# Two orders of TensorE work changed: the matmuls that open an mLSTM head, and two projections that close the token mixing

## The reference

```python
log_w = jnp.where(causal, b[..., :, None] - b[..., None, :] + ig[..., None, :], -jnp.inf)
m_t = jnp.maximum(log_inter, jnp.max(log_w, -1))
w = jnp.exp(log_w - m_t[..., None])
qk = jnp.einsum('bhtd,bhsd->bhts', q, k) * w
```

```python
y = y * lax.rsqrt(jnp.mean(y * y, axis=-1, keepdims=True) + RMS_EPS)
y_ret = (jax.nn.silu(rg) * y) @ w_ret_out
y_na = _neighborhood_attention(na_heads(nq), na_heads(nk), na_heads(nv), rel_bias) @ w_na_out
merged = jax.nn.sigmoid(g_ret) * y_ret + jax.nn.sigmoid(g_na) * y_na
return merged @ w_out
```

## Time and profile before

| | us |
|---|---|
| median of 3 runs | 2721.13 (2720.45 to 2722.01) |
| profiled execution, its own time | 2721.13 |
| its span | 2719.3 |
| TensorE busy (PE) | 2637.1 |
| TensorE weight loads (PEld) | 2344.3 |
| VectorE busy (DVE) | 1584.0 |
| ScalarE busy (ACT) | 1396.6 |

### The profile page before, as it was taken

One profiled execution on the slowest core, in us unless ns is written; L12 is line 12 of the kernel. 1 busy time (PEld: TensorE's weight loads), 2 busy tenths in 40 slices (PEclk: granted clock), 3 DMA queues, 4 the chain that ended last, 5 costly groups with the idle time before them and its releaser, 6 DMA issues.

```text
span 2719.3 us, 46153 instructions
## 1 busy us (share of the span) xinstructions
PE 2637.1 (97%) x16650; PEld 2344.3 (86%) x16650; DVE 1584.0 (58%) x2847; ACT 1396.6 (51%) x2310; POOL 585.7 (22%) x336
## 2 busy tenths in 40 slices
PE   8999999999999998999999999999999999989998
PEld 6789999998888876799999998888869977766996
DVE  3558746675555563449556665555556646545664
ACT  4434567664444444444577654444445445553543
POOL 0007876650000000008866630000000000001000
PEclk9999999999999999999999999999999999999999
DMA  6245554446666653245544446666556655425554
GB/s 215 77 156 171 184 156 140 141 145 200 192 193 193 193 185 110 87 148 183 180 148 140 142 153 204 193 193 193 193 163 196 184 172 178 138 88 163 163 183 149
DMA packets 124037, 447.63 MB, mean 165 GB/s; under 512 B 14280, under 2 KB 14920, under 8 KB 123648
## 3 DMA queue, kind: packets, MB, share of 16 engines
q1 hardware_dynamic: 119808, 434.16, 50.8%
q0 software_dynamic: 2608, 9.08, 1.2%
q10 hardware_dynamic: 1488, 2.59, 0.3%
HBM read 444.74 MB, written 1.05 MB: 164 GB/s over the span
## 4 chain that ended last, share of the span: by engine, by line
PE 92%; DVE 4%; ACT 3%; DMA 1%; issue 1%; ACTq 0%; DVEq 0%
PE ps L748 41%; PE ps L720 14%; PE ps L726 14%; PE ps L723 14%; PE ps L896 4%; DVE X L1574 1%; PE ps L672 1%; PE ps L950 1%; PE ps L867 1%; DVE big L1574 1%; PE ps L782 0%; DMA ring<-in_ffn_in 0%; ACT w_hi L395 0%; DVE stats L1654 0%; DVE X L1650 0%
## 5 line engine op out<-in xcount | busy, mean ns | idle before, releaser
L395 ACT CAST w_hi<-ring 128x1024 fp32r<-128x1024 f32 (+1 forms) x808 | 846.4, 1048 | 999.1 <-PE ps L748 534.3
L407 DVE TENSOR_TENSOR w_lo<-ring,w_hi 128x1024 fp32r<-128x1024 f32 (+1 forms) x629 | 769.2, 1223 | 813.6 <-ACT w_hi L395 805.4
L407 POOL TENSOR_TENSOR w_lo<-ring,w_hi 128x1024 fp32r<-128x1024 f32 (+1 forms) x179 | 429.3, 2399 | 1713.5 <-ACT w_hi L395 1713.5
L720 PE MATMUL ps<-x_hi,w_hi 128*128 128x256 f32 x3104 | 772.8, 287 | 1.7 <-ACT w_hi L395 1.6
L723 PE MATMUL ps<-x_lo,w_hi 128*128 128x256 f32 x3104 | 760.6, 283 | 0.0
L720 PEld LDWEIGHTS ps<-x_hi,w_hi 128*128 128x128 f32 x3104 | 594.1, 191 | 3.3 <-ACT w_hi L395 2.1
L723 PEld LDWEIGHTS ps<-x_lo,w_hi 128*128 128x128 f32 x3104 | 594.9, 192 | 0.0
L726 PE MATMUL ps<-x_hi,w_lo 128*128 128x256 f32 x3104 | 435.7, 283 | 0.0
L748 PE MATMUL ps<-w_hi,x_hi 128*128 128x512 f32 x1488 | 409.7, 394 | 6.0 <-DVE x_lo L1621 1.9
L748 PE MATMUL ps<-w_hi,x_lo 128*128 128x512 f32 x1488 | 404.0, 390 | 0.0
L748 PE MATMUL ps<-w_lo,x_hi 128*128 128x512 f32 x1488 | 402.9, 389 | 0.3 <-DVE w_lo L407 0.3
(11 more groups left out here) (239 smaller groups left out, 1903.2 us busy)
## 6 DMA issues: line engine op xcount, KB each, us to landing
ring<-in_u SPq DMA_DIRECT2D x256, 512.0 KB, 3.5
ring<-in_v SPq DMA_DIRECT2D x256, 512.0 KB, 3.8
ring<-in_ffn_in SPq DMA_DIRECT2D x88, 512.0 KB, 3.5
ring<-in_ffn_out SPq DMA_DIRECT2D x44, 512.0 KB, 3.4
ring<-in_wq SPq DMA_DIRECT2D x32, 512.0 KB, 3.5
ring<-in_ple_gate SPq DMA_DIRECT2D x16, 512.0 KB, 4.3
SC<-in_rows POOLq DMA_DIRECT2D x11, 512.0 KB, 4.8
ring<-in_a_qk SPq DMA_DIRECT2D x8, 512.0 KB, 4.8
```

Of the source, the lines that this page charges most:

```text
L395: nc.scalar.copy(part(w_hi, i)[:, used(name)], tile(i)[:, used(name)]).then_inc(tiles_hi, 1)
L407: eng.tensor_tensor(part(w_lo, i)[:, at], tile(i)[:, at], part(w_hi, i)[:, at], ALU.subtract).then_inc(tiles_low[LOW[n][0]], 1)
L720: mm = nc.tensor.matmul(bank(s)[:, 0:T], hi[:, k, :], x_hi[:, k, :], start=(k == 0), stop=False)
```

## The change

There are two edits.

In `ml_first` the six matmuls are the same, in another order: each half of the decay is followed at once by its mask, the decay bank is reported full, and the scores come last. The second half of the decay now starts its own accumulation.

At the close of the mixing, `ret_out` comes before `na_out`: in the list of loads, in the order of `acc`, and on TensorE, ScalarE and VectorE. ScalarE loads the square root's table (`sqrt_table`: a table load and an activation of one column) before it casts the last tile of `g_na` and tile 0 of `ret_out`, and takes the eight roots before the sigmoid of `g_na`.

```diff
-    + [("na_out", 4), ("ret_out", 8), ("mix_out", 8)]
+    + [("ret_out", 8), ("na_out", 4), ("mix_out", 8)]
...
-             "na_out", "ret_out", "mix_out", "ffn2_out"]
+             "ret_out", "na_out", "mix_out", "ffn2_out"]
...
-                decay, scores = SLOT[("ml", "decay", h)], SLOT[("ml", "scores", h)]
-                slot_free(pe, decay)
-                nc.tensor.matmul(bank(decay)[:, 0:T], ml_sel[0:H8, h, :], ml_rows[0:H8, 7, :], start=True, stop=False)
-                nc.tensor.matmul(bank(decay)[:, T:T + P], ml_sel[0:H8, h, :], ml_rows[0:H8, 7, P:T],
-                                 start=False, stop=False)
-                slot_free(pe, scores)
+                s = SLOT[("ml", "decay", h)]
+                slot_free(pe, s)
+                nc.tensor.matmul(bank(s)[:, 0:T], ml_sel[0:H8, h, :], ml_rows[0:H8, 7, :], start=True, stop=False)
+                nc.tensor.matmul(bank(s)[:, 0:P], ident[:], ml_mask[:], start=False, stop=True)
+                nc.tensor.matmul(bank(s)[:, T:T + P], ml_sel[0:H8, h, :], ml_rows[0:H8, 7, P:T],
+                                 start=True, stop=False)
+                full(nc.tensor.matmul(bank(s)[:, T:T + P], ident[:], ml_mask[:], start=False, stop=True), s)
+                s = SLOT[("ml", "scores", h)]
+                slot_free(pe, s)
                 r, q, k = head_rows(h), h // 2, 4 + h // 2
-                nc.tensor.matmul(bank(scores)[:, 0:T], ml_qk[r, k, 0:P], ml_qk[r, q, :], start=True, stop=True)
-                full(nc.tensor.matmul(bank(scores)[:, T:T + P], ml_qk[r, k, P:T], ml_qk[r, q, P:T],
-                                      start=True, stop=True), scores)
-                nc.tensor.matmul(bank(decay)[:, 0:P], ident[:], ml_mask[:], start=False, stop=False)
-                full(nc.tensor.matmul(bank(decay)[:, T:T + P], ident[:], ml_mask[:], start=False, stop=True), decay)
+                nc.tensor.matmul(bank(s)[:, 0:T], ml_qk[r, k, 0:P], ml_qk[r, q, :], start=True, stop=True)
+                full(nc.tensor.matmul(bank(s)[:, T:T + P], ml_qk[r, k, P:T], ml_qk[r, q, P:T],
+                                      start=True, stop=True), s)
...
+            turn_over("ret", ret_y.rearrange("p t h n -> p t (h n)"))
+            split_to_acc("ret_out", turn="ret")
             moved(pe, SLOT[("na", "out", H8 - 1)])
             to_acc("na_out", tokens(na_oT), 4)
-            turn_over("ret", ret_y.rearrange("p t h n -> p t (h n)"))
-            split_to_acc("ret_out", turn="ret")
...
-                    take_high(act, "g_na", 2 * h + 1)
+                    sqrt_table()
+                    highs("g_na", 2 * h + 1, 2 * h + 2, following="ret_out")
...
+            square_roots(8)
             from_acc("g_na", lambda tb: sig_na[:, tb, :], ACT.Sigmoid)
-            square_roots(8)
-            take_high(act, "ret_out", 0)
             turned_parts("ret")
             highs("ret_out", 1, 8, following="mix_out")
+            acc_here(act, "na_out")
...
-            def gated_from(name, dst, gate):
-
+            turned_parts("ret")
+            lows("ret_out", 1, 8)
+            for name, dst, gate in (("ret_out", merged_tmp, sig_ret), ("na_out", merged, sig_na)):
                 for tb in range(TB):
                     acc_here(dve, name, tb)
                     V.tensor_tensor(dst[:, tb, :], gate[:, tb, :], acc_rows(tb), ALU.mult).then_inc(acc_moved, 1)
-
-            acc_moved_up_to("g_na", TB - 1)
-            gated_from("na_out", merged, sig_na)
-            turned_parts("ret")
-            lows("ret_out", 1, 8)
-            gated_from("ret_out", merged_tmp, sig_ret)
-            acc_moved_up_to("ret_out", TB - 1)
+            acc_moved_up_to("na_out", TB - 1)
```

## The result

The changed kernel takes 2736.89 us (median of 4 runs, 2735.34 to 2738.02) beside 2720.79 us of the kernel before: ratio 1.0053, 95% interval 1.0041 to 1.0066, so it is slower. The medians are 16.1 us apart; the ratio takes in nine more runs of the changed kernel (2729.89 to 2738.33) and stands for 14.4 us. In a second set of runs it was 2736.85 beside 2722.87, ratio 1.0053 (1.0038 to 1.0068). I had forecast +8.6 us and a range up to 2733.5. A few executions far outside all others (2806 us and more) are left out of every ratio and mean.

What follows compares the result with a forecast made beforehand. TensorE, busy for 97% of the span, was taken to bound the kernel. +5.1 us in the mLSTM heads and +3.5 us at the close of the mixing made +8.6 on 2721.13: 2729.7 us, range 2723.5 to 2733.5.

Steps and rivals of the forecast that it cites:

- Part 1, the toll: mLSTM heads (ml_first): three more changes of array rows a head, 0.20 us each at full clock; +5.1 us in all.
- The term for head 0: First mLSTM head, at the lower clock: three more changes of array rows at 0.30 us each, 0.9 us.
- B: mLSTM heads: the toll belongs to the PSUM bank change, not rows; -1.6 us there, 2723.0 in all; chance 0.12.
- C: mLSTM heads: each load overlapping the previous matmul's array rows pays; +0.8 us there, 2725.4 in all; chance 0.05.
- All on TensorE, with nothing beside it: mLSTM heads: the +5.1 us of row changes lies wholly on TensorE, with nothing beside it to hide it.
- Part 2, step 1: Cast of g_na's last tile: the square root's table load ahead of it puts 1.4 us on TensorE's path.
- Step 2: Before ret_out: copy, squares, root, reciprocal and gated halves lead to transposes from 2441.7; ret_out starts at 2444.9 or 2445.7.
- Step 3: ret_out: the clock has the short low stretch, 1.7 us lost, so ret_out ends at 2469.5.
- Step 4: na_out: starts at once after ret_out with a warm clock and takes 14.0 us, to 2483.5.
- Step 5: From na_out's end to mix_out: both products exposed, 2.35 instead of 1.23 us; tail 6.2 us, mix_out at 2489.6.
- D: Close of the mixing: clock falls long after the first pause and again before mix_out's turn; +13.7 us, 2734.8; chance 0.13.

Runs made afterwards that it cites:

- the padded heads: Kernel before with the new mLSTM head order and the decay's matmuls made 128 rows deep by zeros, close of the mixing as before: ratio 1.0003.
- Shifts: Kernel before with 33, 8 or 16 filler matmuls of zeros ahead of the a_v stage: ratios 1.0010, 1.0012 and 1.0010 to the kernel before.
- the swap alone: Changed kernel with the old ml_first, so only ret_out and na_out exchanged against the kernel before: ratio 1.0013.
- the mended kernel: Changed kernel with zeros under the decay, square root's table loaded after the casts, 18 fillers before the retention output's turn: ratio 1.0019 to the kernel before.
- three alignments: The mended kernel with no, 8 or 16 fillers ahead of a_v: ratios 1.0019, 1.0023 and 1.0026 to the kernel before.

## Why the prediction was wrong, point by point

- **Part 1, the toll** (+5.1 us of work): right in its mechanism, 0.5 us too high. Six changes of rows a head, 6.34 us; in the trace seven heads give 7 x 0.59 and head 0 gives 0.51 (72.49 to 73.00 is the start of the next one), 4.6 us. The term for head 0 was 0.9 and is 0.5. Rivals B and C fell with the padded heads.
- **"All on TensorE, with nothing beside it"** is the step that failed. I priced the toll as time alone and put the clock's term in the heads at nothing, because they have no wait; I looked for falls of the clock only behind pauses. The runs showed two falls of 3.4 us, which make two heads 7.94 instead of 6.34 us long: +3.2 us. They are in every trace of the unmended order, and in none where the changes were taken away or the heads filled. The Trainium skill, "TensorE: Matmul & The Clock Gate", Part 1, says that the gate is set by how busy TensorE has lately been; the trace fits it in that 0.54 was granted in heads without a wait, though TensorE's busy time is 3.50 of 3.50 us there, and I had read it as a rule on pauses only.
- **Part 2, step 1:** the wait of 1.4 us is there (1.49 against 0.18). Left out was that it also lets the clock fall in `g_na`'s last tile, 1.6 us with the output matmuls behind it. That, less 0.1 us in each of the wait and the stretch behind it, is 4.87 against 3.5.
- **Step 2** held: reciprocal to transposes, pauses of 4.32 and 0.98 us. **Step 3:** the long low stretch came (2454 to 2461), not the short one that I chose. It cost little more, since TensorE pauses in its first part: `ret_out` took 23.48 instead of 22.07, 1.4 us and not 1.7. The clock was read wrongly here and the sum came out right by luck. **Step 4:** `na_out` at 13.99, forecast 14.0. **Step 5:** tail 6.11, forecast 6.2. The stretch from the last output matmuls to `mix_out` is 52.07 against 50.09: +2.0, forecast +2.1.
- **What no step had:** 4.1 us in stages that the change doesn't touch (2.36 between the heads and the mixing, 1.7 behind it). There the trace after has low stretches at 167, 1041 (twice as long) and 2536 us. 7.84 + 2.36 + 4.87 + 1.7 = 16.8, the spans' difference. The forecast's miss in this trace is thus 8.2 us: 3.2 of clock in the heads less 0.5 of toll, 1.4 at the close, and these 4.1. With the heads and the close right, the forecast would have been 2733.8, just past the end of its range.
- **The rivals:** D had the clock fall again, but ahead of `mix_out`'s turn; the pause there was 2.11 us and the clock stayed up. My range ended at 2733.5 because I gave the clock one place.

**What stays open:** why the untouched stages lose more. Part may be the execution's own: the traces differ by 16.8 us where the means of a set differ by 14.5, and two traces of the changed kernel have falls in different places. Shifts move the clock's share of the kernel before by -2.7 to +1.9 us, and the swap alone showed a fall where its code equals that of before: chance of the moment is part of it. But the mended kernel keeps 5 to 6 us under three alignments, each with an error of about 1. The padded heads alone have +3.1 us already, without a fall in the heads. No experiment separated what in them does that.

## What to carry to other kernels

Order small fp32 matmuls so that the number of array rows changes as seldom as can be, or pad the shallow ones with zeros: a change cost 0.2 us here and hid under nothing. (Padding undid the harm of the new order; the total was no better than before.) When an edit thins TensorE's work or lengthens a pause (by 1.3 us here), price the clock's low stretches as well, some 1.7 us each, even where TensorE never waits. Fillers in six pauses paid more than either edit moved (-12 us); where single runs scatter by 10 us, compare means, beside the kernel before on the same chip, and split each span by its mean clock.

## What the runs showed of the hardware

- The granted clock fell while TensorE was busy without a wait: 3.4 us at 1.2 GHz, twice in eight heads, in all four traces with 6 changes of rows in 6.34 us; not with 4 in 5.93 (one trace), not with 3 in 5.74 (seven traces), not with 2 in 5.54 (five traces), and not with 6 and three fillers more in 6.92 (one trace).
- The toll of a change of rows follows the depth, not the bank: 0.22 us from pair to pair with all depths at 128, 0.42 with 8 and 128 in turn, in the same banks.
- The same code can have low stretches more or fewer, in other places, from one execution to the next: two traces of the changed kernel differ at 1175, 2072.5 and 2444 us. Spans of the kernel before went from 2713.8 to 2724.3 us in one set, with mean clocks of 0.993 to 0.988.
